# Three transformer-like blocks in one program: the order of four mixing stages planned anew from measured step costs

## What is computed

```python
def first_block(...):     # Mamba2 (SSD scan) beside a gated delta rule (GDN), then a SwiGLU feed-forward
    proj = rmsnorm(x, norm_mix_w) @ w_in
    y_ssm = mamba2_mixer(...); y_gdn = gdn_mixer(...)
    merged = sigmoid(gate_ssm) * (y_ssm @ w_proj_ssm) + sigmoid(gate_gdn) * (y_gdn @ w_proj_gdn)
    x = x + merged @ w_out;  x = x + swiglu(rmsnorm(x)) ...
def second_block(...):    # RWKV7 time mixing beside a sparse attention with an index and top-k
    ya = (rwkv7_time_mix(pa, ...) * silu(ga)) @ w_a_out
    yb = (dsa_sparse_attention(q, k, v, iq, ik, iw) * silu(gb)) @ w_b_out
    x = x + gate * ((sigmoid(gm_a) * ya + sigmoid(gm_b) * yb) @ w_o)
def third_block(...):     # feed-forward, then gMLP beside a differential attention, then feed-forward
    x = x + 0.5 * swiglu(...)
    m = sigmoid(g_a) * (y_a @ a_w_proj) + sigmoid(g_b) * (y_b @ b_w_proj)
    x = x + m @ w_out;  x = x + 0.5 * swiglu(...)
```

## Time and profile before

| | |
|---|---|
| median of 3 runs | 3038.27 us (3038.21 to 3054.9) |
| the profiled execution's own time | 3034.87 us |
| its span, first to last instruction | 3033.1 us |
| TensorE busy | 2962.9 us, 98% of the span |
| VectorE, ScalarE, GpSimd busy | 1583.6, 1077.8, 1408.2 us |
| instructions | 42,345 |
| mean granted TensorE clock | 0.993 of full speed |

### The profile page before, as it was taken

One profiled execution on the slowest core, in us unless ns is written; L12 is line 12 of the kernel. 1 busy time (PEld: TensorE's weight loads), 2 busy tenths in 40 slices (PEclk: granted clock), 3 DMA queues, 4 the chain that ended last, 5 costly groups with the idle time before them and its releaser, 6 DMA issues.

```text
span 3033.1 us, 42345 instructions
## 1 busy us (share of the span) xinstructions
PE 2962.9 (98%) x16912; PEld 2381.4 (79%) x16912; DVE 1583.6 (52%) x3162; ACT 1077.8 (36%) x1784; POOL 1408.2 (46%) x1805
## 2 busy tenths in 40 slices
PE   6999999999999999999999999999999999999999
PEld 5778887877888887767877778888877778888887
DVE  5776557565666316559744453333275773333310
ACT  4453334333222223323324432222354554332221
POOL 4554444335555554314333365555444334555553
PEclk9999999999999999999999999999999999999999
DMA  3211212112344422102112222223321112222232
GB/s 127 83 55 64 70 57 65 61 48 94 127 144 147 125 91 67 37 22 70 36 46 73 71 83 97 95 95 100 110 77 63 56 63 91 86 95 97 98 103 85
DMA packets 72069, 248.02 MB, mean 82 GB/s; under 512 B 8128, under 2 KB 8512, under 8 KB 71744
## 3 DMA queue, kind: packets, MB, share of 16 engines
q1 hardware_dynamic: 71872, 245.30, 25.0%
HBM read 243.18 MB, written 2.10 MB: 81 GB/s over the span
## 4 chain that ended last, share of the span: by engine, by line
PE 88%; DVE 9%; ACT 2%; issue 1%; POOL 0%; DMA 0%; SPq 0%; DVEq 0%; ACTq 0%
PE bank L1072 24%; PE bank L1074 24%; PE bank L1073 24%; PE bank L1106 3%; PE bank L1120 3%; PE bank L1569 1%; PE bank L1083 1%; PE bank L1587 1%; PE bank L1578 1%; DVE t L2211 1%; DVE sm L2209 1%; PE bank L1457 1%; PE bank L1112 0%; DVE t L1790 0%; PE bank L1490 0%
## 5 line engine op out<-in xcount | busy, mean ns | idle before, releaser
L2975 POOL TENSOR_TENSOR R<-W,R 128x256 fp32r<-128x256 f32 x1715 | 1301.4, 792 | 1510.0 <-ACT R L2573 1509.9
L1072 PE MATMUL bank<-u,R 128*128 128x512 f32 (+1 forms) x3440 | 1389.5, 404 | 13.3 <-DVE u L1746 3.2
L1074 PE MATMUL bank<-u,R 128*128 128x512 f32 (+1 forms) x3440 | 1347.4, 392 | 0.0
L1073 PE MATMUL bank<-u,R 128*128 128x512 f32 (+1 forms) x3440 | 1345.4, 391 | 0.0
L1072 PEld LDWEIGHTS bank<-u,R 128*128 128x128 f32 (+1 forms) x3440 | 648.1, 188 | 160.5 <-issue 11.0
L1074 PEld LDWEIGHTS bank<-u,R 128*128 128x128 f32 (+1 forms) x3440 | 646.9, 188 | 141.7 <-issue 0.8
L1073 PEld LDWEIGHTS bank<-u,R 128*128 128x128 f32 (+1 forms) x3440 | 648.8, 189 | 128.0 <-issue 5.0
L2573 ACT ACTIVATE R<-W 128x1024 fp32r<-128x1024 f32 (+2 forms) x452 | 451.3, 1005 | 140.1 <-PE bank L1074 132.7
L2603 ACT ACTIVATE u<-t 128x512 fp32r<-128x512 f32 x126 | 78.3, 630 | 305.7 <-DVE t L1768 249.6
L1779 DVE SCALAR_TENSOR_TENSOR X<-bank,X 128x512 f32<-128x512 f32 x32 | 22.1, 692 | 239.0 <-PE bank L1074 239.0
L1754 DVE TENSOR_TENSOR t<-bank,t 128x512 f32<-128x512 f32 x66 | 45.5, 689 | 174.4 <-PE bank L1074 164.5
(11 more groups left out here) (395 smaller groups left out, 2741.1 us busy)
## 6 DMA issues: line engine op xcount, KB each, us to landing
W<-in_in SPq DMA_DIRECT2D x48, 512.0 KB, 3.3
W<-in_ff_in SPq DMA_DIRECT2D x44, 512.0 KB, 3.3
W<-in_g_qkv SPq DMA_DIRECT2D x24, 512.0 KB, 3.3
W<-in_ada SPq DMA_DIRECT2D x24, 512.0 KB, 3.3
W<-in_f1g SPq DMA_DIRECT2D x22, 512.0 KB, 3.3
W<-in_f1u SPq DMA_DIRECT2D x22, 512.0 KB, 3.2
W<-in_f2g SPq DMA_DIRECT2D x22, 512.0 KB, 3.2
W<-in_f2u SPq DMA_DIRECT2D x22, 512.0 KB, 3.2
```

The costliest lines, as they stand in the source:

```text
L1072: e.matmul(b[0:cols, :], wh, hi, start=(k == 0), stop=False)
L1073: e.matmul(b[0:cols, :], wh, lo, start=False, stop=False)
L1074: i = e.matmul(b[0:cols, :], wl, hi, start=False, stop=(k == KT - 1))
L2975: i = e.tensor_tensor(R[q % NH][:, 1024 + a:1024 + b], W[p % NW][:, a:b], R[q % NH][:, a:b].bitcast(F32), SUB)
```

## The change

It replaces numbers in `SEG` and nothing else. Every entry keeps its engines and the order of its parts; no step, instruction, buffer or semaphore rule is added or removed. The durations now come from a trace of the kernel, and `sums` gets the whole distance between its steps. Since `weave` reads the table, the order of the parts in the engine queues changes in all four stages; the other parts of the program keep theirs. The core of the diff:

```diff
-    dense="p1.36", sums="p.32 v2.0 s.69", xd="p.43 v.68", bt="p.43 s.6", cb="p.86 v.68", st0="v1.7", st="p.86 v1.14",
-    ch="p.23 v.68", che="s2.1", cm="v.75|g1.3", sz="s.6 v.69", sy="p1.6 v1.6", sn1="s.63", sn1p="p.25", sn2="v2.7", sn2p="p.45", sn3="v.74",
...
-    hos="p.43", ho2="v.74", hz="s.6 v.69", conv="s.72 v2.24", conv2="s.63 v.75", gate="s.6", branch="v.7", part="v1.4", sh="s.69 v.74", wd="s.63",
-    ru="p1.2 s1.37", r1="v2.3 s.63", r1p="p.2", r2="v2.6", r2p="p1.72", r3="v2.3", r3p="p.86", r3b="v1.38", r4="v4.4|s1.9",
-    rm="p1.1 v1.38", rt="p.43 s.6", rz="g1.05", s1="p.43 s.27", s2="p.22 v.29", s4="p.43 v1.0", s3="p.54", ry1a="s.6",
-    ry1="p.86 v.69", ry2a="s.62", ry2="p.2", ry2n="v2.6", ry3p="p1.72", ry3="v3.0", rg="s.63", ixp="s.6", ixw="p.05 v.2",
-    ixs="p.64 s.5 v.6", ixt="v1.2", ax="s.6", ap="s.6", av="p.43 s.6", an0="p.86", an1="s1.18", an2="v5.2", an2p="p.43",
-    an3="s.68", sa="p1.1 v1.37 s1.48", sb="v1.0", sc="p.27 s.43", sd="p.72", dg="s.6 v.69", do_="v.69", frq="p.86 v2.3", fr="p.86 v2.4",
...
+    dense="p1.4", sums="p0.39 v3.4 s2.4", xd="p0.42 v0.65", bt="p0.42 s0.6", cb="p0.81 v0.65", st0="v2.12", st="p0.58 v1.19", ch="p0.27 v0.73",
+    che="s1.68", cm="v1|g1.39", sz="s0.58 v0.65", sy="p1.84 v1.58", sn1="s0.62", sn1p="p0.85", sn2="v3.14", sn2p="p1.11", sn3="v0.67",
...
+    hos="p0.44", ho2="v0.72", hz="s0.6 v0.62",
+    conv="s0.68 v2.27", conv2="s0.57 v0.77", gate="s0.61", branch="v0.92", part="v1.52", sh="s0.67 v0.72", wd="s0.63", ru="p1.06 s1.25",
+    r1="v2.83 s0.63", r1p="p0.83", r2="v3.51", r2p="p1.02", r3="v2.34", r3p="p0.88", r3b="v1.63", r4="v4.24|s1.67", rm="p1.02 v1.24",
+    rt="p0.45 s0.54", rz="g0.99", s1="p0.58 s0.27", s2="p0.38 v0.29", s4="p0.6 v1.08", s3="p0.73", ry1a="s0.57", ry1="p0.68 v0.69", ry2a="s0.63",
+    ry2="p0.81", ry2n="v2.08", ry3p="p1.02", ry3="v3.42", rg="s0.58", ixp="s0.58", ixw="p0.34 v0.19", ixs="p0.87 s0.49 v0.61", ixt="v1.23",
+    ax="s0.6", ap="s0.59", av="p0.38 s0.51", an0="p0.86", an1="s1.07", an2="v5.63", an2p="p0.36", an3="s0.68", sa="p0.73 v1.35 s1.52", sb="v1.02",
+    sc="p0.26 s0.41", sd="p0.63", dg="s0.6 v0.59", do_="v0.66", frq="p0.74 v2.08", fr="p0.52 v2.24", ft1="s0.54 v0.48", ft1s="s0.52", ft1p="p0.84",
+    ft2="v4", ft2r="s1.26", ft3="v1.58", fc1="p0.85", fc2="v2.8", fc3="p0.84", fc4="v0.75", gv="s0.9", gu="s1.89", gvt="p0.48 s0.67",
...
```

More of the change, by code:

```diff
@@ L293 @@
 SEG = {k: [[(x[0], float(x[1:])) for x in part.split("|")] for part in v.split()] for k, v in dict(
-    dense="p1.36", sums="p.32 v2.0 s.69", xd="p.43 v.68", bt="p.43 s.6", cb="p.86 v.68", st0="v1.7", st="p.86 v1.14",
-    ch="p.23 v.68", che="s2.1", cm="v.75|g1.3", sz="s.6 v.69", sy="p1.6 v1.6", sn1="s.63", sn1p="p.25", sn2="v2.7", sn2p="p.45", sn3="v.74",
-    pair="s.63 v.75", hq="p.86", hqs="s1.2", hn="v6.9", hnp="p.43", hn2="s.6", hg="p.23 v1.38 s1.23", hb="p.23 v1.5",
-    eq="p.43 s.6", ek="p.43 s.6", ea="v1.6", eb="v3.2", ec="v1.0", ep="p.43 s.6", hu="p1.72 v1.38", i0="g1.3|p.43 s.6 v1.5", il="p.55 s.6", ix="p.43 v.69", iu="p.43 s.6", ip="p.55 v.69", it="p.43 s.6", iq="g1.28", im="p.55 v.69",
@@ L298 @@
-    in_="p.55 v.65", hk="p.5 v2.0", hs1="p.22 v.35", hs2="p.22 s.28", hs3="p.54 v.33", ho="s.36", hon="v4.0",
-    hos="p.43", ho2="v.74", hz="s.6 v.69", conv="s.72 v2.24", conv2="s.63 v.75", gate="s.6", branch="v.7", part="v1.4", sh="s.69 v.74", wd="s.63",
-    ru="p1.2 s1.37", r1="v2.3 s.63", r1p="p.2", r2="v2.6", r2p="p1.72", r3="v2.3", r3p="p.86", r3b="v1.38", r4="v4.4|s1.9",
-    rm="p1.1 v1.38", rt="p.43 s.6", rz="g1.05", s1="p.43 s.27", s2="p.22 v.29", s4="p.43 v1.0", s3="p.54", ry1a="s.6",
@@ L302 @@
-    ry1="p.86 v.69", ry2a="s.62", ry2="p.2", ry2n="v2.6", ry3p="p1.72", ry3="v3.0", rg="s.63", ixp="s.6", ixw="p.05 v.2",
-    ixs="p.64 s.5 v.6", ixt="v1.2", ax="s.6", ap="s.6", av="p.43 s.6", an0="p.86", an1="s1.18", an2="v5.2", an2p="p.43",
-    an3="s.68", sa="p1.1 v1.37 s1.48", sb="v1.0", sc="p.27 s.43", sd="p.72", dg="s.6 v.69", do_="v.69", frq="p.86 v2.3", fr="p.86 v2.4",
-    ft1="s.6 v.45", ft1s="s.63", ft1p="p.86", ft2="v4.1", ft2r="s.63", ft3="v1.5", fc1="p.2", fc2="v3.6", fc3="p.45", fc4="v.74", gv="s.6", gu="s.6", gvt="p.43 s1.13",
@@ L306 @@
-    gn="v1.5 s.73", gnn="v5.7", gn2="v1.5", gs="p1.72 v1.5").items()}
+    dense="p1.4", sums="p0.39 v3.4 s2.4", xd="p0.42 v0.65", bt="p0.42 s0.6", cb="p0.81 v0.65", st0="v2.12", st="p0.58 v1.19", ch="p0.27 v0.73",
+    che="s1.68", cm="v1|g1.39", sz="s0.58 v0.65", sy="p1.84 v1.58", sn1="s0.62", sn1p="p0.85", sn2="v3.14", sn2p="p1.11", sn3="v0.67",
+    pair="s0.61 v0.77", hq="p0.86", hqs="s1.09", hn="v6", hnp="p0.38", hn2="s0.52", hg="p0.28 v1.58 s1.08", hb="p0.31 v1.37", eq="p0.41 s0.6",
+    ek="p0.35 s0.6", ea="v1.49", eb="v3.2", ec="v1.95", ep="p0.52 s0.49", hu="p1.74 v1.24", i0="g1.41|p0.48 s0.53 v1.58", il="p0.57 s0.58",
@@ new lines @@
+    ix="p0.48 v0.63", iu="p0.51 s0.59", ip="p0.56 v0.65", it="p0.53 s0.6", iq="g1.27", im="p0.55 v0.65", in_="p0.57 v0.59", hk="p0.53 v1.91",
+    hs1="p0.21 v0.34", hs2="p0.22 s0.27", hs3="p0.52 v0.22", ho="s0.35", hon="v4.82", hos="p0.44", ho2="v0.72", hz="s0.6 v0.62",
+    conv="s0.68 v2.27", conv2="s0.57 v0.77", gate="s0.61", branch="v0.92", part="v1.52", sh="s0.67 v0.72", wd="s0.63", ru="p1.06 s1.25",
+    r1="v2.83 s0.63", r1p="p0.83", r2="v3.51", r2p="p1.02", r3="v2.34", r3p="p0.88", r3b="v1.63", r4="v4.24|s1.67", rm="p1.02 v1.24",
@@ L307 @@
+    ft2="v4", ft2r="s1.26", ft3="v1.58", fc1="p0.85", fc2="v2.8", fc3="p0.84", fc4="v0.75", gv="s0.9", gu="s1.89", gvt="p0.48 s0.67",
+    gn="v1.47 s0.67", gnn="v4.24", gn2="v1.96", gs="p1 v1.47").items()}
 EVACUATE = ("conv", "sz", "hz", "gate", "branch", "part", "sh", "ax", "ap", "dg", "gv", "gu", "ixp", "ixw", "ixs", "gvt", "gs")
```

## The result

| | before | after |
|---|---|---|
| median | 3039.24 us (3036.98 to 3054.90, 19 runs) | 3051.95 us (3047.94 to 3055.12, 19 runs) |
| ratio after to before, 95% interval | | 1.0035 [1.0026, 1.0045] |
| profiled execution: its time, its span | 3034.87, 3033.1 us | 3053.64, 3051.8 us |
| mean granted clock of it | 0.993 | 0.989 |

The change makes the kernel slower, by 0.35%. The forecast was 3028 us and faster; its range ended at 3050. The ratio compares the runs otherwise than by the quotient of the two medians (1.0042), so the two can differ by a few us; the difference of the mean times is 9.4 us.

The account below looks back on a forecast made before the run. TensorE, busy for 2962.9 of 3033.1 us, was taken as the bound. Terms of -3 - 1 - 4 - 4 + 2 = -10 us took the profiled 3034.9 to 3025, forecast as a median of 3028, range 3008 to 3050.

Parts of the forecast that it names:

- What bounds the kernel: Whole kernel: TensorE is busy for 2962.9 of 3033.1 us, leaving 70.2 us idle, 35.5 of it in the four mixing stages.
- The ceiling: Four mixing stages: a perfect order could win 35.5 us of idle time and 15.1 of clock, together 50.6 us, 1.7%.
- the one on the costs: Mixing stages: the new table's ratio of TensorE to chain time was called better, the old about 4% too small in stages one to three.
- Time-step sums: First stage: the 3.48 us wait at 52.93 should go, partly handed back at the stage's end; -3 us, ends 0 and -5.2.
- Second stage: Second mixing stage: dense steps left for its end against tighter chains of four heads; -1 us, bounds -9 and +6.
- Third: Third mixing stage: the burst of index scores may move to a better or worse place; -4 us, ends -10.8 and +7.
- the burst: Third stage: index scores run together, with 4.2 us of waits and 6.6 of clock; a coin's throw on 10.8 us.
- Fourth: Fourth mixing stage: with 32 dense steps left over, every wait removed is won; -4 us, ends -12 and +5.
- New waits: New waits in new places: bounded by zero and 35.5 us, taken at +2 us beyond the stage terms.
- C: Rival: slower, TensorE reaches chain steps early and the clock falls; one more such place 3049 us, two 3060; chance 0.17.
- B: Rival: gains are given back, or durations don't carry over to a new order; 3038 us, from 3034 to 3042; chance 0.26.
- Busy time: TensorE's busy time: a move of more than 5 us would mean that breaking up dense runs has a price, put at nothing.

Follow-up runs that it names:

- e6: Old durations for TensorE's parts, new ones for VectorE, ScalarE and GpSimd, against the kernel before: 3033.91 us, ratio 0.9977.
- f17: Old table with only the dense step's cost raised from 1.36 to 1.40 us in stages two to four, against the kernel before: 3040.87 us, ratio 1.0000.
- e9: New table with a dense step at the old 1.36 us in stages two to four, against the kernel before: 3045.48 us, ratio 1.0030.
- e1: New table in the first mixing stage only, old table in the other three, against the kernel before: 3035.99 us, ratio 0.9976.
- e2: New table in the second mixing stage only, old table elsewhere, against the kernel before: 3045.30 us, ratio 1.0019.
- e3: New table in the third mixing stage only, old table elsewhere, against the kernel before: 3044.72 us, ratio 1.0006.
- e4: New table in the fourth mixing stage only, old table elsewhere, against the kernel before: 3045.75 us, ratio 1.0016.
- f18: Old table with new TensorE durations of the chain steps in stages two to four, dense kept at 1.36, against the kernel before: 3039.39 us, ratio 1.0000.
- e8: Old table with one number moved, dense 1.36 to 1.38 us, against the kernel before: 3042.70 us, ratio 1.0007.
- e10: New table with a dense step at 1.32 us in stages two to four, against the kernel before: 3028.69 us, ratio 0.9980.
- f15: New table with a dense step at 1.30 us in stages two to four, against the kernel before: 3047.35 us, ratio 1.0004.

## Why the prediction was wrong

**What bounds the kernel** held: all of the loss is in the four stages. The ceiling of 35.5 us of idle time and some 15 of clock was not contradicted; the best order at full clock (e6) gains 8 us (3002.1 for 3009.7).

**The step that failed** is the one on the costs: "On the whole the new ratio of TensorE to chain time is the better one", with its conclusion that "the old plan put too many dense steps between two chain steps". I had compared the table's sum for a stage with the trace's busy time (611 and 636 against 647.9; the 531 against 573.9 of the third stage is 7.5% short and not 8%), and taken the nearer sum for fewer waits. f17 shows the step to be wrong at full clock: with a dense step at 1.40 and nothing else changed, the plan for stages two and three comes nearer to the busy time, idle TensorE rises by 7.0 us and the full-clock time by 7. e9, which takes this entry back in the new table, wins 5.5 of the 6.4 us again. By the trace 1.40 is even nearer to what a dense step takes in the stages (1.47 in the mean), so a truer number made a worse plan. Why it did stays open; that an underrated filler gives the chains slack is a reading and not shown. The conclusion that the old plan put too many dense steps between two chain steps has nothing behind it.

**Time-step sums**, -3 with ends 0 and -5.2: the wait at 52.93 went, as foreseen, and was handed back, at 49.48 and 210.20. In the profile the stage is as long as before (210.9 for 210.3). Run alone (e1) it is faster, ratio 0.9976, median 2.8 us lower. The term is right in sign and near in size (2.3 us at full clock), but by luck: the wait that was to go had only moved, and e1's profile has 71.2 us of idle time for 70.2. Where the gain comes from isn't shown.

**Second stage**, -1 with ends -9 and +6: +4.0 in the profile, +2.9 at full clock alone (e2). **Third**, -4 with ends -10.8 and +7: +8.9 in the profile, outside, but +3.7 at full clock alone (e3); the burst, on which I put a coin's throw, stands some 12 us earlier in the stage, with the same three waits and 0.55 over 18 us where it had 0.53 over 14. In both orders the last 13 scores stand back to back, though dense work was free to run between them: the dense steps of `gm` wait for nothing, and the order has the rest of them (six of the eight tiles before, all eight now) only behind the last score. `weave` takes a filling list only if it can start earlier (`x[0] < stream[0]`), and a score and a dense step can both start when the next bank comes free, so the score wins each tie, whatever the costs. That I could have read from the code. **Fourth**, -4 with ends -12 and +5: +8.2 in the profile, outside, and nothing at full clock alone (e4); `sc` waits 7.7 us instead of 3.5, only partly offset by `ft1p` (1.8 for 3.9), and the clock fell behind some of them. **New waits**, taken at +2 near the low end of their bounds: idle TensorE in the stages rose by 9.1 us net, so this term was the one sized worst.

**The rivals.** What C says of the outcome came true (chain steps for which TensorE waits, the clock falling behind), with a mean time 9.4 us above before, near its one-place case of 11. But it wasn't one place with a run of low clock. The waits that grew are small and spread out: those of `sc` by 4.2 us over eight places, of the norm root by 2.5, and more of the kind for the rest of the 8.5; the lower clock added a third. B's second half, durations that don't carry over, was not the main thing but did happen. The new VectorE, ScalarE and GpSimd durations, `r2` at 3.51 among them, did no harm over TensorE's old ones (e6). But the wait of 2.57 us at 2550.03, with 0.72 over the 12 us behind it (3.4 us lost), is there because the norm's operations took 6.22 us beside GpSimd where they take 2.44 without it. This is what the rule of the Trainium skill, page "SBUF — State Buffer", section "Who interferes with whom", would lead one to expect, that VectorE and GpSimd hold a shared port pair one at a time. The trace agrees with it here, as at `r2` in the earlier trace rows.

**Busy time** moved by more than the 5 us that I had named. It was not a price of breaking up dense runs: at full clock the part that isn't idle is 2938.1 us for 2940.2. The 10.2 us are the lower clock's.

**What stays open.** Why a dense step at 1.40 costs 3 to 7 us at full clock. Whether the clock loss, which hides f17's loss in measured time, goes with the order. The chain steps' TensorE durations do nothing on the old table (f18, 3009.7), while with the new durations of the other engines they go with 9.2 us (e9 3011.3, e6 3002.1); those two differ in stage one as well. I can't say how much of it is these durations and how much is the accident of one order, since two hundredths in one number (e8) cost 4 us. For the same reason e6 (0.9977), e1 (0.9976) and e10 (the lowest median, 3028.69, with an interval that reaches 1) are candidates rather than proofs of a better table: they are the best of eighteen.

## What to carry to other kernels

That a plan's total agrees better with the busy time, or one entry with the trace, is no proof that the plan is better: here the filler's cost was moved nearer to what it takes, and the kernel lost at full clock. Try the filler's cost by itself, below its measured mean too, since slack for the chains may be worth more than a true number. When a new wait appears, look at what the other engines did beside the operation waited for before the cost table is blamed. Where new costs reshuffle a whole order, try the entries in groups (by engine, by stage) before the table as a whole: here the durations of three engines gained 8 us at full clock and those of TensorE lost more than that.

## What the runs showed of the hardware

The clock loss of one and the same program varies more than the change: e10 was timed from 3021 us (clock 0.995) to 3053 us (0.983), and f15, with the third lowest full-clock time (3004.3), has a mean 11 us above e10's (a median 19 us above), 9.3 of them clock loss (38.1 against 28.8 us). Multiplying each span by its granted clock brings the standard deviation of e10 from 11.4 us to 2.3 and that of f15 from 11.6 to 2.7.

Waits of 2.6 to 3.6 us at 49.48, 210.20 and 2550.03 were followed by a clock of 0.70 to 0.72 over windows of 10 to 12 us that begin near their ends, as the one at 52.93 was before (0.72 over 6 us). The wait of 2.48 us at 704.28 was not: its window shows 1.00. TensorE had worked without a wait for 5 us or more before each of these. So waits of about the same length cost their length alone, or about twice as much.

The same small VectorE operations of a norm took 2.44 us alone and 6.22 beside GpSimd's weight splitting.

Matmuls of 512 columns follow each other every 0.227 us (1.36 / 6). The Trainium skill, page "TensorE: Matmul & The Clock Gate", section "Wait — 56ns, not 53.3ns?", gives 215.7 ns for them back to back at the full clock; the trace differs, and here the measurement decides.
